# GpSimd takes three of six low halves of the branch, and tile 2's first transposes go ahead of the last gate job, in a four-layer decoder trunk

## The reference

```python
q, k, v, g, a = _split(h @ w_in, [...])
o, s = gla_recurrence(q * DK ** -0.5, k, v, logf, s0)     # causal, in chunks of 64 tokens
o = rmsnorm(o, g_on)                                      # per head, 256 wide
return (o * silu(g)) @ w_out, s                           # then y = y + this
```

## Time and profile before

| what | us |
|---|---|
| median of 3 runs (lowest to highest) | 1153.78 (1153.21 to 1155.95) |
| time of the profiled execution | 1151.64 |
| its span, first to last instruction | 1149.9 |
| TensorE busy in it | 1112.4 (97%) |
| VectorE, ScalarE, GpSimd busy | 675.2, 494.7, 383.1 |
| end of layer 0 (`sequence(7)` to the last low half) | about 208 to 230 |
| end of layer 3 | about 1075 to 1097 |

### The profile page before, as it was taken

The page is one execution under the profiler, slowest core; times in us unless marked ns, Lnnn a source line. Parts: engine busy times, 40 slices in busy tenths (PEclk is TensorE's granted clock), DMA queues, the critical chain, the costliest instruction groups (busy, mean ns, idle before and its releaser), DMA issues. The chain is left out here.

```text
span 1149.9 us, 25599 instructions
## 1 busy us (share of the span) xinstructions
PE 1112.4 (97%) x10579; PEld 974.7 (85%) x10579; DVE 675.2 (59%) x1215; ACT 494.7 (43%) x968; POOL 383.1 (33%) x321
## 2 busy tenths in 40 slices
PE   7999999899999999999999999999999999999897
PEld 6889888899758988879945499999999889888796
DVE  6462255854999779777444555595544362255742
ACT  6542376643443322222354553322553451466643
POOL 5545213243313423114300134453354245312230
PEclk9999999999999999999999999999999999999999
DMA  5335233333314787884789923224220335233302
GB/s 169 103 111 165 92 111 113 127 84 99 118 50 153 241 277 235 275 311 138 255 326 407 383 74 106 64 89 130 80 75 3 111 110 165 75 129 111 100 30 78
DMA packets 127787, 168.81 MB, mean 147 GB/s; under 512 B 20384, under 2 KB 93480, under 8 KB 127663
## 3 DMA queue, kind: packets, MB, share of 16 engines
q1 hardware_dynamic: 115609, 152.59, 39.9%
q10 hardware_dynamic: 12062, 14.59, 3.6%
HBM read 150.70 MB, written 16.81 MB: 146 GB/s over the span
## 5 line engine op out<-in xcount | busy, mean ns | idle before, releaser
L737 POOL TENSOR_TENSOR w_lo<-raw,w_hi 128x512 fp32r<-128x512 f32 (+2 forms) x267 | 360.7, 1381 | 688.8 <-ACT w_hi L1501 688.7
L773 PE MATMUL psum<-h_hi,w_hi 128*128 128x272 f32 x1616 | 471.2, 292 | 6.6 <-DVE h_lo L2425 4.7
L775 PE MATMUL psum<-h_hi,w_lo 128*128 128x272 f32 x1616 | 467.3, 289 | 0.0
L774 PE MATMUL psum<-h_lo,w_hi 128*128 128x272 f32 x1616 | 464.8, 288 | 0.0
L773 PEld LDWEIGHTS psum<-h_hi,w_hi 128*128 128x128 f32 x1616 | 303.3, 188 | 20.2 <-issue 15.3
L774 PEld LDWEIGHTS psum<-h_lo,w_hi 128*128 128x128 f32 x1616 | 303.7, 188 | 0.1
L775 PEld LDWEIGHTS psum<-h_hi,w_lo 128*128 128x128 f32 x1616 | 303.0, 187 | 0.0
L1501 ACT ACTIVATE w_hi<-raw 128x1024 fp32r<-128x1024 f32 (+1 forms) x137 | 135.5, 1034 | 116.8 <-PE psum L775 79.5
L773 PE MATMUL psum<-w_hi,h_hi 128*128 128x512 f32 (+2 forms) x352 | 124.1, 353 | 1.2 <-DVE dsa_score_s L2519 0.8
L775 PE MATMUL psum<-w_hi,h_lo 128*128 128x512 f32 (+2 forms) x352 | 121.0, 344 | 1.8 <-issue 1.8
L774 PE MATMUL psum<-w_lo,h_hi 128*128 128x512 f32 (+2 forms) x352 | 121.0, 344 | 0.7 <-issue 0.7
(11 more groups left out here) (331 smaller groups left out, 1366.2 us busy)
## 6 DMA issues: line engine op xcount, KB each, us to landing
smp_keys<-in_cache_k_dram SPq DMA_DIRECT2D x128, 256.0 KB, 4.9
raw<-in_gla_w_in_dram SPq DMA_DIRECT2D x23, 1024.0 KB, 5.4
spare<-in_cache_v_dram SPq DMA_DIRECT2D x36, 512.0 KB, 7.2
raw<-in_dsa_w_in_dram SPq DMA_DIRECT2D x17, 1024.0 KB, 5.3
raw<-in_cache_v_dram SPq DMA_DIRECT2D x28, 512.0 KB, 8.7
gla_s_in<-in_state_gla_dram SPq DMA_DIRECT2D x16, 512.0 KB, 7.9
raw<-in_gla_w_out_dram SPq DMA_DIRECT2D x8, 1024.0 KB, 6.7
out_dram<-gla_s_in ACTq DMA_DIRECT2D x16, 512.0 KB, 4.6
```

The costliest lines, as they stand in the source:

```text
L737: pool.tensor_tensor(copies(key, pair_view(w_lo, key)[:, k]), raw_copies(key, k), copies(key, pair_view(w_hi, key)[:, k].bitcast(F32)), AL ...
L773: pe.matmul(out, lh, rh, start=start, stop=False)
L774: pe.matmul(out, lh, rl, start=False, stop=False)
L775: return pe.matmul(out, ll, rh, start=False, stop=stop)
```

## The change

Five things change, in both GLA layers.

1. The low halves of pieces (0,0), (1,0) and (0,1) move from VectorE to GpSimd, in its queue ahead of the low half of the second output weight. They signal `pool_done`; the output projection and the reuse of `tmp_og` wait for it.
2. The transposes of piece (2,0) go ahead of `gate_job(15)`. Their bank becomes 6 instead of 3, and that of (2,1) becomes 3 instead of 6.
3. VectorE does `piece(2)` ahead of `gate_part(15)` (which scales the last gate job's result), `low(2)` right behind it, and then pieces 3, 4 and 5 without a low half between.
4. ScalarE does `branch_hi(2)` ahead of the last silu, with a wait for the gate job (which still reads those columns of `h_hi`).
5. ScalarE's two halves of the split of (`out`, 1) both stand behind `branch_hi(5)`.

A semaphore is also renamed (`gate_mul` to `pool_done`).

```diff
+POOL_LOWS = ((0, 0), (1, 0), (0, 1))
@@ GpSimd's queue, ahead of the low half of the second output weight
+                if KINDS[key[0]] == 0 and key[1:] == ("out", 1):
+                    hi, lo = H[key[0] % 2]
+                    for t, half in POOL_LOWS:
+                        k = slice(4 * half, 4 * half + 4)
+                        pool.wait_ge(*on("h_hi", (key[0], "out"), t, half))
+                        pool.tensor_tensor(lo[:, k, cols(t)],
+                                           GLA[key[0]][7][:, OUT_PIECES.index((t, half)) % 4]
+                                           .rearrange("p (k t) -> p k t", k=4),
+                                           hi[:, k, cols(t)].bitcast(F32), ALU.subtract)\
+                            .then_inc(*sig("pool_done", (key[0], "out"), t, half))
@@ TensorE: ready() of the output projection
                         pe.wait_ge(*on("h_lo", (L, "out"), 2, k // 4))
+                        pe.wait_ge(*on("pool_done", (L, "out"), 1 - k // 4, k // 4))
@@ TensorE: banks of out_transposes, and its call ahead of the last gate job
-                b = {(0, 0): 4, (1, 0): 5, (2, 0): 3, (0, 1): 4, (1, 1): 5, (2, 1): 6, (3, 0): 3, (3, 1): 4, (SMP, 1): 5}[t, half]
+                b = {(0, 0): 4, (1, 0): 5, (2, 0): 6, (0, 1): 4, (1, 1): 5, (2, 1): 3, (3, 0): 3, (3, 1): 4, (SMP, 1): 5}[t, half]
@@
                         out_transposes(L, 1, 0)
+                        out_transposes(L, 2, 0)
                     gate_job(4 * t + 5 if t < NP_T - 1 else 15)
-                for t, half in OUT_PIECES[2:6]:
+                for t, half in OUT_PIECES[3:6]:
@@ ScalarE
                 branch_hi(1)
+                act.wait_ge(*on("proj", (L, "g", KT - 1), 1))
+                branch_hi(2)
                 gate(L, gate_g, KT - 1, ("gate_dve", (L, "g", KT - 1), 1))
-                branch_hi(2)
                 branch_hi(3)
-                split_hi(pair_of[(L, "out", 1)], (0,))
                 branch_hi(4)
                 branch_hi(5)
-                split_hi(pair_of[(L, "out", 1)], (1,))
+                split_hi(pair_of[(L, "out", 1)])
                 act.preload_act_table_set(EXP_LN)
@@ VectorE
                     if i >= 4:
-                        dve.wait_ge(*on("h_lo", (L, "out"), *OUT_PIECES[i - 4]))
+                        old = OUT_PIECES[i - 4]
+                        dve.wait_ge(*on("pool_done" if old in POOL_LOWS else "h_lo", (L, "out"), *old))
                     gated(*OUT_PIECES[i], tmp_og[:, i % 4])
@@
                 piece(1)
-                low(0)
-                low(1)
+                piece(2)
                 gate_part(15)
-                piece(2)
+                low(2)
                 piece(3)
-                low(2)
                 piece(4)
-                low(3)
                 piece(5)
                 low(4)
                 low(5)
```

More of the change, by code:

```diff
@@ L743, in _ @@
                         pool.tensor_tensor(gate_d[:, k, :], gate_d[:, k, :], rstd[:], ALU.mult)\
-                            .then_inc(*sig("gate_mul", key[0], k))
+                            .then_inc(*sig("pool_done", key[0], k))
         @block.tensor
@@ L1911, in projected @@
                             for q in (k - 3, k - 2):
-                                gate(L, gate_d, q, ("gate_mul", L, q))
+                                gate(L, gate_d, q, ("pool_done", L, q))
                 def sample_exp(grp):
```

## The result

The changed kernel is slower: 1161.39 us (median of 4 executions, 1157.13 to 1162.80) against 1153.64 us (4 executions, 1153.21 to 1155.95), a ratio of 1.0052 with the interval 1.0036 to 1.0068. The profiled execution of the changed kernel is the fastest of its four: 1157.13 us, span 1155.4 us. That is 5.49 us above the profiled execution before (1151.64, span 1149.9).

The account below looks back on a forecast made before the run. TensorE, busy 97% of the span, was taken to bound the kernel. Per layer, new waits of 5.78 less 2.60 gone gave about 3.17 us; two layers add 6.3 to 1153.78, forecasting 1160.1 us, range 1156.3 to 1162.6.

Parts of the forecast that it names:

- last gate job, waiting for the third piece: TensorE's last gate job starts 2.53 us later, 2.10 idle, until VectorE has read the third piece from bank 6.
- first half of `first_two`: Output projection's first half starts 1.38 us later; a wait of 0.36 replaces that of 1.07.
- second half: Second half of `first_two` starts 0.55 us later; a wait of 0.70 replaces that of 1.53.
- transposes of tile 3: TensorE starts them 3.17 us later per layer, after waiting 2.62 us for VectorE's normalisation.
- both layers, on the profiled time: Layers 0 and 3 each lose 3.17 us, 6.3 us in all, 5.8 to 8.8 by the bounds.
- The wait at bank 6: Before the last gate job: it shares bank 6 with piece (2,0)'s transposes, so TensorE idles 2.10 us.
- The two short waits: TensorE waits 0.36 and 0.70 us before the two halves of `first_two`.
- the dear end of the unknown: GpSimd's low half of the branch takes twice the assumed 1.26 us, and the layer costs 4.4 us.
- The tail: Late table load puts the last rows' root beside GpSimd's weight block, held instruction by instruction; tile 3's transposes 3.17 us late.
- The rival that is held up less: At tile 3's root: one or none of GpSimd's instructions in its way; 2.6 to 4.0 us slower; chance 0.15.
- The hidden root: Squares run early, so only the second half's shift is left, 2 x 0.55 us; 1154.9; chance 0.08.
- the faster case: Taking low halves off VectorE wins both waits, 2 x 2.60 us, giving 1148.6; chance 0.05.

Follow-up runs that it names:

- bank3: Changed kernel with the last gate job writing bank 3 instead of 6 and the transposes of (2,1) in bank 6; median 1158.25 us, ratio 1.0031.
- late_split: Changed kernel with the second half of ScalarE's split of the second output weight moved behind the root; median 1160.93 us, ratio 1.0065.
- narrow_w: Changed kernel with GpSimd's low half of the output weight's second half worked out for 16 columns only; median 1156.46 us, ratio 1.0020.
- norm_first: As root_first, with the whole normalisation of tile 3 moved in front of the first piece; median 1155.95 us, ratio 1.0017.
- root_first: As bank3, with tile 3's root split from the sample's and taken early, VectorE's four lines before the first piece; median 1155.73 us, ratio 1.0008.
- two_heads_first: As root_first, with tile 3's normalisation for two of four heads moved in front of the first piece; median 1152.86 us, ratio 0.9988.

## Why the prediction was right, step by step

The forecast was 1160.1 us; the median came to 1161.39, inside the range, and slower was the side with 0.80. Its steps, each as a delay against the kernel before, counted from the first transposes of layer 3:

| step | predicted | measured |
|---|---|---|
| last gate job, waiting for the third piece | 2.53 | 3.28 - 0.85 = 2.43 |
| first half of `first_two` | 1.38 | 8.22 - 6.81 = 1.41 |
| second half | 0.55 | 11.88 - 11.44 = 0.44 |
| transposes of tile 3 | 3.17 | 18.85 - 16.05 = 2.80 |
| both layers, on the profiled time | 6.3 | 5.49 |

*The wait at bank 6* was right in cause and nearly in size. Of the 2.43 us, 0.63 are there in `bank3` too (its gate job starts 1.48 us after the first transposes, 0.85 before): they go with the four transposes that now run first, for which the forecast has 0.43. The wait itself is the other 1.80, forecast 2.10, and `bank3` shortens the stage by as much, 1.78 us.

*The two short waits* (0.36 and 0.70 forecast) came as 0.34 and 0.40. GpSimd's low half takes 1.30 us where I took 1.26; the dear end of the unknown did not come.

*The tail* was right in its mechanism and mis-sized: **3.17 should have been 2.80**. Two numbers of that step were off, and one reading. I let GpSimd's weight block wait for `low(5)` and end at 1093.45, which is 1096.08 here; it ended at 1095.81, 0.27 earlier. The reading: I had the wrong lines held. I had read the hold as one of "an instruction with two inputs in SBUF", so the root's first line, with one input, would run free and the third be held. It is the first that took 1.26 us, and the third took 0.17. The block's end decides in either case, and VectorE's normalisation ended 2.13 us after it, as forecast, so the wrong lines changed nothing in the sum. The other 0.10 is the step from there to TensorE, taken as 0.15 and here 0.05 (1097.94 to 1097.99). But the reading was too narrow, and the kernel before had a sign of it: line 2344, with one input, took 0.25 us there beside the block, and 0.16 in most of its other runs. The Trainium skill ("SBUF — State Buffer", section "Who interferes with whom") lists `tensor_scalar` among the operations that can take the shared ports; the trace agrees, with 1.26 us here, 0.94 in `late_split`, and 0.17 in `narrow_w`, where GpSimd's block is short.

*The rival that is held up less* had its chance by the phase of the two engines. `late_split` shows why it didn't come even when I tried to make it: what the root is spared, the normalisation pays. *The hidden root* and *the faster case* are refuted by the two waits themselves.

*What the prediction left out* is the clock. It has no term and no rival for it, though it puts two pauses of 2 us or more into a TensorE that had none longer than 1.4 us at this place. The 0.8 us by which the stages were priced too high and the 2 us by which the median exceeds them have opposite signs; without the first the forecast would have been nearer the profiled execution, and further from the median. The side, the place and the cause were forecast; that the median came within 1.3 us is in part luck.

## What to carry to other kernels

Before a result is moved ahead of other work in an in-order queue, look at what it writes (a bank that the next job in line also needs) and at what is pushed back behind it on the other engines: here a root that ran just clear of GpSimd's block fell into it. A short chain of VectorE instructions with their inputs in SBUF, beside a GpSimd block, can cost one GpSimd instruction for each of its own (pieces that read one input from PSUM kept their 0.68 us), so taking work off the chain's front doesn't help while its end is still inside the block; place the chain, or part of it, where GpSimd is idle. And price a pause of TensorE of 2 us or more at more than its length: 5 falls of 1.7 us behind 12 pauses are 0.7 us for each.

## What the runs showed of the hardware that I had not expected

TensorE's clock fell to its lower level behind 5 of 12 pauses of 2.0 to 2.2 us in front of tile 3, and behind one of 2.0 us in `norm_first`, at a price of 1.7 us where I added it up. Behind the 1.75 us pause at the gate job no profile of these kernels shows one (0 of 10, in five profiles). The same kernel has the fall in one execution and not in the next.

The falls at 510:520 are of the same kind. In layer 1 TensorE has a pause there whose length differs from profile to profile. In seven profiles it is 1.87 to 2.56 us, and behind six of these the clock falls (not behind the 2.56 us of `bank3`); in the others it is 1.83 us or less, in the kernel before and the changed one among them, and none shows a fall. Nor is there one behind a pause of 2.15 us at 591 us in the kernel before. In `root_first`, the pause and the slice after it:

```profile
510.68 0.29 PE L786 MATMUL psum<-w_hi,h_lo 128*128 128x256 f32 x1 [2.16 <-issue]
```

```profile
511.00:512.00 1.00, 1.00 (x8) 1.00 (x7) 0.96 (x2) 0.00 (x0) 0.00 (x0) 0.60 1.01 386
```

The falls at 50:60 (7 of 14 profiles) and 920:930 (2) have no such pause in front, only one of 0.53 us at 48 us; their cause stays open.

The Trainium skill ("TensorE: Matmul & The Clock Gate", section "HAM oscillation — how this bites in real kernels") describes waits between bursts of matmuls after which each burst starts at the lower clock. The traces here agree in kind, but the pauses are shorter, from 1.87 us on, and the fall comes only in some executions.

VectorE and GpSimd take turns, instruction by instruction, where both read SBUF. Four normalisations of 0.42 us beside four subtractions of 1.26 took 5.46 us (`root_first`), two beside the same block 2.63 (`two_heads_first`); a small `tensor_scalar` on 5 elements per partition took 1.26 us instead of 0.16, because it waited for its turn.
